# A transformer kernel's attentions, rebuilt as head pairs in steps of two query blocks, with GpSimd dividing

## The reference

```python
x = x + 0.5 * swiglu(rms_norm(x, ffn1_norm), ffn1_w_in, ffn1_w_out)
proj = rms_norm(x, mix_norm) @ w_mix_in
# 8 heads: keys within 128 positions, a sink logit per head
m = maximum(logits.max(-1), s); p = exp(logits - m)
p = p / (p.sum(-1) + exp(s - m)); o_a = einsum('bgrqk,bkgd->bqgrd', p, v_a)
# 8 heads: three softmaxes over the same queries
o_cmp, o_sel = nsa_cmp_sel(...)     # 31 compressed keys; selected blocks (here all causal keys)
o_win = banded_attention(...)       # window of 512: all causal keys
o_b = gates[0] * o_cmp + gates[1] * o_sel + gates[2] * o_win
x = x + concat(o_a, o_b) @ w_mix_out
x = x + 0.5 * swiglu(rms_norm(x, ffn2_norm), ffn2_w_in, ffn2_w_out)
# second block, layer 0: 16 heads with a relative bias and a mask by chunks of 64
# layer 1: 16 heads of a latent attention (64 plain + 32 rotary dimensions), the same mask
p = softmax(s, axis=-1); o = einsum('bhqk,bkhd->bqhd', p, v); h = h + g1 * (o @ wo)
# after each attention a convolution feed-forward of width 2816
```

## Time and profile before

| | us |
|---|---|
| median of three runs (lowest, highest) | 2562.7 (2558.75, 2564.5) |
| the profiled execution, own time | 2569.69 |
| its span | 2568.2 |
| PE busy, share of the span | 2452.8, 96% |
| DVE, ACT, POOL busy | 1296.1, 1055.8, 106.1 |
| granted PE clock, mean over the span | 0.949 of full speed |

### The profile page before, as it was taken

The page is one execution under the profiler, slowest core; times in us unless marked ns, Lnnn a source line. Parts: engine busy times, 40 slices in busy tenths (PEclk is TensorE's granted clock), DMA queues, the critical chain, the costliest instruction groups (busy, mean ns, idle before and its releaser), DMA issues.

```text
span 2568.2 us, 33704 instructions
## 1 busy us (share of the span) xinstructions
PE 2452.8 (96%) x12124; PEld 1988.0 (77%) x12124; DVE 1296.1 (50%) x2173; ACT 1055.8 (41%) x1731; POOL 106.1 (4%) x236
## 2 busy tenths in 40 slices
PE   6999999989999999999999989999998898999998
PEld 5888877867667888888787778788777677887876
DVE  5654655343455434435534466556456444664554
ACT  4323324342454432342424645335344373552452
POOL 2100210000000000001000000000000000000000
PEclk9999999965789999999999999999999799999999
DMA  6854953240001335626432123233222102233322
GB/s 205 269 171 145 330 187 106 84 95 21 9 9 50 82 90 172 196 82 200 144 99 70 51 66 98 83 106 90 74 77 64 59 2 66 68 87 105 93 81 98
DMA packets 265799, 268.56 MB, mean 105 GB/s; under 512 B 8879, under 2 KB 210157, under 8 KB 265709
## 3 DMA queue, kind: packets, MB, share of 16 engines
q1 hardware_dynamic: 239997, 187.20, 24.7%
q0 software_dynamic: 21584, 78.08, 9.1%
q10 hardware_dynamic: 4128, 2.10, 0.4%
HBM read 265.17 MB, written 12.66 MB: 108 GB/s over the span
## 4 chain that ended last, share of the span: by engine, by line
PE 89%; DVE 6%; ACT 3%; issue 2%; DMA 0%; ACTq 0%; DVEq 0%; SPq 0%
PE bank L325 14%; PE bank L327 14%; PE bank L326 14%; PE bank L331 10%; PE bank L333 9%; PE bank L332 9%; PE bank L1274 4%; PE bank L1295 3%; PE bank L1411 3%; PE bank L1285 2%; PE bank L1422 2%; PE bank L1433 2%; DVE w_lo L308 1%; PE bank L1676 1%; PE bank L541 1%
## 5 line engine op out<-in xcount | busy, mean ns | idle before, releaser
L325 PE MATMUL bank<-xT_hi,w_hi 128*128 128x512 f32 x1552 | 608.9, 392 | 17.6 <-DVE w_lo L308 8.9
L308 DVE TENSOR_TENSOR w_lo<-raw,w_hi 128x2048 fp32r<-128x2048 f32 (+3 forms) x202 | 414.8, 2056 | 395.5 <-ACT w_hi L304 394.7
L326 PE MATMUL bank<-xT_lo,w_hi 128*128 128x512 f32 x1552 | 605.5, 390 | 0.0
L327 PE MATMUL bank<-xT_hi,w_lo 128*128 128x512 f32 x1552 | 605.5, 390 | 0.0
L304 ACT ACTIVATE w_hi<-raw 128x2048 fp32r<-128x2048 f32 (+3 forms) x202 | 348.0, 1724 | 490.3 <-PE bank L333 465.3
L325 PEld LDWEIGHTS bank<-xT_hi,w_hi 128*128 128x128 f32 x1552 | 292.4, 188 | 84.8 <-DVE w_lo L308 11.4
L327 PEld LDWEIGHTS bank<-xT_hi,w_lo 128*128 128x128 f32 x1552 | 292.3, 188 | 61.6
L326 PEld LDWEIGHTS bank<-xT_lo,w_hi 128*128 128x128 f32 x1552 | 292.4, 188 | 59.5
L331 PE MATMUL bank<-w_hi,hid_hi 128*128 128x512 f32 x704 | 275.5, 391 | 8.1 <-DVE w_lo L308 8.1
L333 PE MATMUL bank<-w_hi,hid_lo 128*128 128x512 f32 x704 | 274.6, 390 | 0.0
L332 PE MATMUL bank<-w_lo,hid_hi 128*128 128x512 f32 x704 | 274.5, 390 | 0.0
(11 more groups left out here) (272 smaller groups left out, 3242.7 us busy)
## 6 DMA issues: line engine op xcount, KB each, us to landing
raw<-in_ffn_w_in_dram SPq DMA_DIRECT2D x40, 1024.0 KB, 6.2
raw<-in_f_win_dram SPq DMA_DIRECT2D x40, 1024.0 KB, 6.0
mod_w<-in_mod_w_dram POOLq DMA_DIRECT2D x48, 512.0 KB, 5.4
mod_w_more<-in_mod_w_dram POOLq DMA_DIRECT2D x48, 512.0 KB, 5.7
raw<-in_ffn_w_out_dram SPq DMA_DIRECT2D x24, 768.0 KB, 4.5
raw<-in_f_wout_dram SPq DMA_DIRECT2D x24, 768.0 KB, 4.5
raw<-in_a_wqkv_dram SPq DMA_DIRECT2D x12, 1024.0 KB, 5.1
skewed_strips<-bias_strips POOLq DMA_DIRECT2D x32, 320.0 KB, 6.2
```

Source lines behind the costliest of these rows:

```text
L308: dve.tensor_tensor(out=w_lo[:, slot, :n], in0=raw[:, slot, :n], in1=w_hi[:, slot, :n].bitcast(f32), op=ALU.subtract).then_inc(lo_done, 1)
L325: pe.matmul(o, lhsT=w[0], rhs=xs[0], start=first, stop=False)
L326: pe.matmul(o, lhsT=w[0], rhs=xs[1], start=False, stop=False)
L327: return pe.matmul(o, lhsT=w[1], rhs=xs[0], start=False, stop=last)
```

## The change

All attentions become objects of one rebuilt `PairAttention`.

- A step holds two query blocks of both heads, (3, 0) first and then (2, 1), so four units: with all causal keys 512, 512, 128, 128 columns, then 384, 384, 256, 256; banded 256, 256, 128, 128, then four of 256. A group is such a pair of steps. The banded attention is 4 groups, the mixed one 4 groups of five steps (two for the selected branch, two for the window branch, and one `Windows` step for the compressed keys of all blocks). The first block thus has 28 steps, the other two 16 each.
- In an iteration PE issues the scores of step k, the transposes of step k-1 and the values of step k-2. The scores take banks 0 to 3, the transposes banks 4 to 6, all values bank 7.
- GpSimd multiplies the probabilities by the inverse sums before they are transposed, and in the mixed attention by the gate too. `rows_pe`, ACT's copy of the rows and DVE's multiplication go; the branches add up in PSUM. DVE's work grows by a copy of the middle bank of transposes in each step and by two small reciprocals for one.
- The first block's queries and keys are now kept as high and low parts (three passes, the low parts made by DVE in the projection), its output arrives as high and low parts of `q0`, and `MixT` and `mix` go.
- The compression's matmuls go from 128 of 62 columns to 32, behind 16 additions that GpSimd makes ahead of the attention, and stand in the attention's PE iterations 3 and 4; the rest of it in iterations 5 to 9 of PE, ACT and DVE. Its weights are half the size, and ACT issues none of the load.

```diff
@@ PairAttention @@
-            def pe(self, pe):
-                for step in range(self.steps + 3):
-                    if step < self.steps:
-                        self.scores_pe(pe, step)
-                    if 0 <= step - 2 < self.steps:
-                        self.transposes_pe(pe, step - 2)
-                    if 0 <= step - 3:
-                        self.values_pe(pe, step - 3)
-                        if (step - 3) % TOK == TOK - 1:
-                            self.rows_pe(pe, (step - 3) // TOK)
+            def pe(self, pe, beside={}):
+                for k in range(len(self.steps) + 2):
...
+            def transposes_pe(self, pe, k):
...
+                        pe.wait_ge(self.n, self.after("n", k, i + 1))
...
+            def values_pe(self, pe, k):
...
+                if k in self.first and k:
+                    pe.wait_ge(self.l, self.g0 + self.first[k])
...
+            def act(self, act, beside={}):
...
+                        self.exps_act(act, k, (0, 1))
+                    if k - 2 in self.last:
+                        g = self.last[k - 2]
+                        act.wait_ge(self.o, self.after("o", k - 2))
+                        act.activation(self.hi[:, g, :], bank[7][:, :], ACT.Copy).then_inc(self.h, 1)
...
+                        self.exps_act(act, k, (2, 3))
...
+            def dve(self, dve, beside={}):
...
+                    if k - 2 in self.last:
+                        g = self.last[k - 2]
+                        dve.wait_ge(self.h, self.g0 + g + 1)
+                        dve.tensor_tensor(out=self.lo[:, g, :], in0=bank[7][:, :], in1=self.hi[:, g, :].bitcast(f32),
+                                          op=ALU.subtract).then_inc(self.l, 1)
+                    if step and step.windows is None and step.sink is None:
+                        dve.wait_ge(self.e, self.after("e", k, 2))
+                        dve.reciprocal(self.inverses(k, 0, 2), self.sums(k, 0, 2)).then_inc(self.r, 1)
+                    if 1 <= k <= len(self.steps):
+                        self.copies(dve, k - 1, "dve")
...
+                    elif step.sink is None:
+                        dve.reciprocal(self.inverses(k, 2, 2), self.sums(k, 2, 2)).then_inc(self.r, 1)
...
+            def pool(self, pool):
...
+                    for i, unit in enumerate(step.units):
+                        p = self.prob(k, unit)
+                        pool.wait_ge(self.r, self.after("r", k, i // 2 + 1))
+                        if step.gate is None:
+                            ins = pool.tensor_scalar(p, p, self.inverses(k, i), None, ALU.mult)
...
+        PAIRS_OF_BLOCKS = ((3, 0), (2, 1))
```

More of the change, by code:

```diff
@@ L19 @@
 N_CMP = SEQ // CMP_STRIDE - 1
+CMP_W = N_CMP + 1
 WINDOW_A = 128
@@ L1541, in tokens @@
             return slice(qi * P, (qi + 1) * P)
-        banded, mixed = [], []
-        for h in range(HEADS_A):
-            g = h // GROUP
-            for qi in range(TOK):
-                first = max(0, qi - 1)
-                keys = (qi + 1 - first) * P
-                banded.append(dict(
-                    parts=[(qT[half(h), h // 2, tokens(qi)], kT[half(h), K_A + g, first * P:first * P + keys])],
-                    n=keys, bias=tables[:, h % 4, SEQ - keys:SEQ], first=neg_sink[:, h:h + 1], sink=h,
-                    values=[v_tok[:, t, V_A, :] for t in range(first, qi + 1)], own=g * DH,
-                    gate=None, to=mix[:, qi, h * DH:(h + 1) * DH], add=None, t=h,
-                    table=table_ready(h) if qi == 0 else None))
@@ L1579, in three, with steps_of, group_of @@
         def three(q, k):
             return [(q[0], k[0]), (q[1], k[0]), (q[0], k[1])]
+        PAIRS_OF_BLOCKS = ((3, 0), (2, 1))
+        def steps_of(unit, **how):
+            return [Step([unit(par, qi) for qi in blocks for par in range(2)], **how) for blocks in PAIRS_OF_BLOCKS]
+        def group_of(steps, tables, loads, **more):
+            for step in steps:
+                step.loads, step.masks = [], []
+            full_ = [step for step in steps if step.windows is None]
+            full_[-1].loads = loads
+            return dict(steps=steps, tables=tables, **more)
@@ new lines, in window_scores_pe @@
+        def window_scores_pe(pe, p, done):
+            g = 2 * p // GROUP
+            w = slice(g * CMP_W, (g + 1) * CMP_W)
+            pe.wait_ge(c_kc, 1)
+            for qi in range(TOK):
+                both = [three([x_[half(par), 4 + p, tokens(qi)] for x_ in (q0_hi, q0_lo)],
+                              [x_[half(par), w] for x_ in (kc_hi, kc_lo)]) for par in range(2)]
+                for m in range(3):
+                    for par in range(2):
+                        q, key = both[par][m]
+                        ins = pe.matmul(bank[par][:, qi * CMP_W:(qi + 1) * CMP_W], lhsT=q, rhs=key, start=m == 0, stop=m == 2)
+                        if qi == TOK - 1 and m == 2:
+                            ins.then_inc(done, 1)
@@ L1700, in cmp_act, with cmp_sd_act @@
+        def cmp_sd_act(act):
             act.wait_ge(c_mean, 1)
[L1701 to L1712 removed]
@@ L2266, in program @@
         proj = Projection(A["w_mix_in"][0], norm_mix)
-        mixT_1 = MixT(mix, att_mixed.done)
-        out_1 = MixOut(A["w_mix_out"][0], mixT_1.done)
+        out_1 = MixOut(A["w_mix_out"][0], att_1, None, q0_hi, q0_lo)
         norm_ffn2 = Norm(out_1.x_ready, column("ffn2_norm", KT))
```

890 lines of the change are left out of this document (475 added, 415 removed).

## The result

The changed kernel takes 2500.8 us (2498.6 to 2501.7, four runs) against 2560.7 for the kernel before; the ratio is 0.9764, 95% interval 0.9747 to 0.9781. It is faster, by 60 us and not by the 173 that were forecast, and 2500.8 lies outside the range of 2355 to 2450.

The account below looks back on a forecast made before the run. PE was taken as the bound (busy 96%, 89% of the chain); first block -147, chunked -9.5, latent -17 and projection +1 sum to -172.5 us: 2397.2 profiled, 2390 as median, range 2355 to 2450.

Parts of the forecast that it names:

- GpSimd's multiplication: In all pair steps: 0.8 us for 512 columns, 0.5 for 256, 0.28 for 128; bounds 0.54 and 1.14 for 512.
- Rival 2: GpSimd late in all 28 pairs: at 1.14 us for 512 columns, each about 1 us longer, 2418 us; chance 0.15, shut-out included.
- 2.8 lengths a pair of steps: GpSimd's share of the ring: two long and two half-long pieces, some 2.8 lengths of 512 columns a pair.
- The ring: PE's loop of waits through DVE, ACT and GpSimd over two steps: 7.8 us a chunked group, 9.6 a latent one.
- 34 + 10: First block: 34 us for four banded groups at 8.5 each, and 10 for the compression.
- The Windows step: Mixed attention: a string of eight short instructions with its scores and transposes, 3.8 us a group.
- Start of the first block: Projection ahead of the first block: low parts of the three-pass queries on DVE add 1 us (0 to 3).
- Rival 1: PE's clock stays low in the first block: -104 us in place of -147, 2433 us; chance 0.15.
- Rival 2's other half: GpSimd doesn't work while DVE does: about 1.8 us a pair, 50 in all, 2440 us; chance 0.15, late GpSimd included.
- Rival 3: First block waits for the compression's 16 GpSimd additions: at 2.5 us each, 17 us later, 2407 us; chance 0.05.
- Rival 4: Kernel slower than before: GpSimd's multiplications set the pace of all 28 pairs, from 3.0 us for 512 columns; chance 0.03.
- the signs of being wrong: First block's stretch ends before 650 or after 705 us, or a latent group takes over 10.6 us.

Follow-up runs that it names:

- e13: Changed kernel with only ACT's high part moved behind all four exponentials and DVE's low part behind the second reciprocal; 2434.1 us, ratio 0.9502 to the kernel before.
- e7: e2 with all exponentials ahead of high part and copies on ACT, both reciprocals ahead of copy and low part on DVE; 2388.6 us, ratio 0.9297.
- e2: Changed kernel with the immediate 1.0 as second factor in GpSimd's one-scalar multiplication; 2418.4 us, ratio 0.9423 to the kernel before.
- e10: e7 with GpSimd's multiplication back in the changed kernel's one-scalar form; 2424.9 us, ratio 0.9456 to the kernel before.
- e6: e2 without the four Windows steps, leaving out the compressed branch's attention; 2400.1 us, ratio 0.9350 to the kernel before.
- e8: Changed kernel with six thrown-away matmuls of 128 columns more in each PE iteration from the third on; 2496.5 us, ratio 0.9721 to the kernel before.
- e9: e2 with 72 GpSimd instructions of several forms more, one after the other, behind its last work for the latent attention; one execution, 2421.8 us.

## Why the prediction was wrong

- **GpSimd's multiplication** is the first step that failed: "I take 0.8 for 512", with 1.14 as the upper bound from four times a select of 128 columns. It is 1.56 in the one-scalar form and 0.69 to 0.77 with a second factor. The upper bound was none: the select and the memset are other instructions, and nothing in the trace before said what this form costs. Rival 2 named the mechanism, its price was too small: "about 1 us longer", where the chunked group came out 5.7 above the forecast. By the prediction's own 2.8 lengths a pair of steps, 1.56 in place of 0.8 adds 2.1 us, an estimate that makes the chunked group 9.9; the other 3.6 are the next point. The figure that the Trainium skill gives ("GPSIMD Engine Reference", 3.1 Elementwise), 769 ns for 512 elements, agrees with the two-scalar form (766 in the mixed attention) and not with the one the change uses.
- **The ring** is the second, and it made the first so dear. It was "7.8" for bias, exponentials, reciprocal, GpSimd, transposes, values, scores *two steps on*. The low part was in it as 0.7 us on DVE ("the second comes at 4.1"). I priced the instruction and not its wait. It waits for the high part, that for the values of step k-2, which PE issues behind the transposes of step k-1, which wait for GpSimd. So in every second step GpSimd's whole work lies between PE's values and PE's next transposes, not beside them. e13 shows it: with those two instructions moved and nothing else, 67 us are back by the ratios, and the chunked group is 10.1 in place of 13.5. In the fast form the whole order of e7 brings some 30 (e2 against e7); the two parts alone were not moved there. The sum also had no term for GpSimd's own work as a bound, which is what holds e10's group at 10.1.
- With both mended, the rings come out as forecast. In e7 a chunked group takes 7.84 us (forecast 7.8), a latent one 9.5 (9.6), out_1 starts at 672.7 (673.6), the whole takes 2388.6 (2390). The account of what PE has to do, and of the two-step ring, was right for a kernel in which this wait is not there. That out_1's start and the whole agree to 1 us is in part luck: the three stretches are shorter than forecast (128.9 against 135, 71.2 against 75.4, 86.6 against 92.0, most of the last two in their starts and ends), and the rest of the kernel is 8.5 us longer in e7's profile, 5.1 of it ahead of the first scores. By the ratio, 0.9297 against a forecast of 2390 / 2562.7 = 0.9326, e7 is some 7 us better, which its interval doesn't tell apart.
- The banded attention and the compression took 58.4 us from first scores to the mixed attention's, 41.9 in e7; the forecast of 34 + 10 counts from the first bias, 4 us behind the first scores. It is 42.2 with the form alone (e2) and 52.5 with the order alone (e10), so here it was the form.
- The Windows step: 3.8 forecast, 4.6 by e6. Start of the first block: +1 forecast, +4.8 measured (three memsets of the compression, 0.8, and the low parts).
- Rival 1, the low clock: the clock did stay at 0.61 and 0.87 in the first block's two halves and fell to 0.75 in the chunked stretch. In the second block e8 gives it back for at most 0.9 us a group; in the first block its price is not shown. With the form alone it rises to 0.81 and 0.93 there, without any filler (e2).
- Rival 2's other half, GpSimd shut out by DVE, did not happen: 1562 ns alone, 1557 in the attention, and DVE's bias of 512 columns still 0.69. By the rule of the Trainium skill ("SBUF — State Buffer", Who interferes with whom) it was not to be expected in these loops, and the trace agrees: the one-scalar form never took more than 1566 ns there.
- Rival 3: GpSimd's 16 additions ran from 523.1 to 535.8, 0.72 us each; nothing waited for them. Rival 4 stayed away for the whole, but it is what happened in the second block, 32 and 11 us slower, at half the price per instruction that I had put as its threshold. The threshold was that of the whole kernel, with the first block's 147 us in it. Worked out for the second block alone, from the same ring, it is 0.8 + 9.5 / 8 / 2.8 = 1.2 us for the chunked attention and 0.8 + 17 / 8 / 2.8 = 1.6 for the latent one, an estimate: even the ring as forecast would have lost time in the chunked attention at 1.56 and gained next to none in the latent one.
- Of the signs of being wrong both came: out_1 started at 707.3, behind 705, and a latent group took 13.7, over 10.6. Transposes were released by GpSimd as said.

## What to carry to other kernels

Price an instruction of an engine that the trace doesn't show in its very form (number of operands and operations), or give the upper bound as unknown; a neighbour of another kind bounds nothing. For each instruction that is put into a loop, follow its wait back through the other engines' order: if it leads back to the engine that waits for it within the same iteration, that iteration is serial, whatever the lags say. Put what waits for old results behind what makes the next ones. Try such an order and a faster instruction together as well as apart: here each hid a part of what the other was worth.

## What the runs showed of the hardware

- On GpSimd, a multiplication by one scalar takes longer than one by two factors (a scalar and an immediate 1.0): 1562 against 693 ns for 512 columns, 603 against 372 for 128. Slopes are 2.5 and 0.84 ns a column.
- DVE can hold GpSimd up. In e9 one multiplication of 128 columns, 372 ns at its least, took 2283 from 1994.5 on, while DVE ran a weight split with two inputs in SBUF until 1996.5; the split itself took 2.34 us, against 2.29 elsewhere:

```profile
L2452 POOL TENSOR_SCALAR cT<-cT,ones x3: 372/378/2283, 1993.5 to 1994.5; 128x128 f32<-128x128 f32 x3
```

```profile
1994.19 2.34 DVE L320 TENSOR_TENSOR w_lo<-raw,w_hi 128x2048 fp32r<-128x2048 f32 x1 [11.09 <-ACT w_hi L316]
```

The Trainium skill ("SBUF — State Buffer", Who interferes with whom) says that such a DVE instruction contends with a GpSimd instruction that reads SBUF; this row agrees. In the attentions DVE reads one side from PSUM, and no such stretching is seen.
- A PE kept busy with thrown-away matmuls was granted a higher clock (0.77 to 0.92) and finished little sooner where another engine set the pace (seven chunked groups 85.8 us against 87.7).
